# Gated DeltaNet and attention in one core: X^T of the inversion's levels 1 to 4 by VectorE's 32x32 transposes, and attention's matmuls in an order that alternates the halves of the array

## The chip, the cores and the metric

The kernel is one program on one NeuronCore of a Trainium2 chip. The metric is the device time in microseconds of one execution; lower is better. Engines are named as the profile names them: PE is TensorE's matmuls, PEld its weight loads, DVE is VectorE, ACT is ScalarE, POOL is GpSimd, SP is SyncE.

## What is computed

One inference step of a two-layer trunk, for 512 prompt tokens and 8 sequences of 8 sampled tokens (576 tokens together, 2048 channels). Layer 0 projects the normed input and splits the columns among sliding-window attention and a gated DeltaNet with 8 heads. The part of the DeltaNet that matters here solves, for each head and each chunk of tokens, a unit lower triangular system; the attention part is plain softmax attention with sinks.

```python
# gated DeltaNet, per head and chunk
lower = jnp.tril(jnp.einsum('...id,...jd->...ij', kb, kc) * decay, -1)
a_mat = lower + jnp.eye(c, dtype=f32)
sol = lax.linalg.triangular_solve(a_mat, rhs, left_side=True, lower=True, unit_diagonal=True)
...
# attention of the prompt, by blocks of 128 queries against 256 keys
s = jnp.einsum('...qhgd,...khd->...hgqk', q, k).astype(jnp.float32) * (HD_A ** -0.5)
...
return jnp.einsum('...hgqk,...khd->...qhgd', p.astype(v.dtype), v)
```

Layer 1 is a convolution module with its own projections; the change doesn't touch it.

## The kernel before

All activations lie with the channels on the partitions. The frame of the whole program is a stream of projection tiles: 133 weight tiles of 2048 x 128, each multiplied with the 576 tokens in 96 matmuls (16 blocks of 128 channels, 3 products of a high and a low part, 2 halves of the tokens). `proj(m, s, e)` issues one eighth of a tile: 12 matmuls with 288 columns. The weights are split on the chip: ACT writes `w_hi`, DVE writes `w_lo`.

Everything else of layer 0 is hung between these eighths by hand. `PE_PLAN` says after which eighth (slot) of a head's four tiles TensorE issues which step of the previous head's DeltaNet; `DVE_PLAN` and `ACT_PLAN` say at which slot VectorE and ScalarE come to theirs. The order on each engine is therefore fixed by the code, and semaphores that count steps (`pe_head`, `dve_head`, `act_head`, `pool_head`) connect the engines. Heads 0 and 7 are written out, heads 1 to 6 run in a loop of three rounds with two heads each.

The triangular matrices are inverted by doubling. X and its transpose are kept side by side in `xx[:, 0]` and `xx[:, 1]`, as four chunks of 128 x 128. After level l, X is block diagonal with blocks of 2^(l+1). Level l has three steps on TensorE, each with one eighth of a projection tile (12 matmuls) between it and the next:

- `a{l}` (L658): M_l times X, 4 matmuls of 128 columns, into bank 1 of `gp`. It waits for DVE's `X{l-1}`. ACT then copies it to `a1` (step `A{l}`).
- `x{l}`: the update of X, 4 matmuls of 64 columns with X^T as the weights (L666, bank 2, levels 1 to 5), and at once the update of X^T, 4 matmuls of 64 columns with `a1` as the weights (L669, bank 3, levels 1 to 6).
- DVE's `X{l}` subtracts both updates from the halves of `xx` that they touch (L1380, `full<-full,gp` of 128x256).

So `a{l}` and `x{l}` stand at every second slot, from slot 7 on. Between its `X{l}` steps DVE has the taps of the next head's short convolution (`arena<-arena,small`) and the `w_lo` halves.

Prompt attention has 16 units, each spread over three slots. In `att_scores` (L826) the two heads of a pair sit in partitions 0 to 63 and 64 to 127, so that a matmul uses 64 rows of the array; the first half's matmuls all go before the second half's, and each half writes its own bank. `att_turn` (L838) transposes the previous unit's probabilities, `att_weigh` (L846) multiplies them with V, with 64 columns of weights for either half. The weighing of the sampled tokens (L890 with the cached values, 128 rows; L892 with the new values, 8 rows) runs over the 8 sequences for one half of the columns and then for the other.

A float32 matmul is one instruction in the code and two in the trace (two weight loads and two matmuls).

Of the kernel before, what the change touches and what calls it, by code (L numbers as in the profile page):

```python
# [20 lines left out]
P = 128  # L21
# [58 lines left out]
class Tally:  # L80
# [15 lines left out]
    def leave(self, rounds):  # L96
# [5 lines left out]
LV = range(1, LEVELS)  # L102
PE_HEAD = (["kv_tok", "gcum", "norm", "gram", "m0"] + [f"{s}{i}" for i in LV for s in ("a", "x")]
           + ["u0", "so0"] + [f"{s}{c}" for c in range(1, NC) for s in ("s", "u", "so")] + ["o_chan"])
DVE_HEAD = (["kg", "dmask", "ssum", "vs", "Mt", "attn", "X", "Xt"] + [f"X{i}" for i in LV]
            + ["vp0", "S0", "o0"] + [f"{s}{c}" for c in range(1, NC) for s in ("r", "vp", "S", "o")]
            + ["on", "y"])
ACT_HEAD = ["sq", "decay"] + [f"A{i}" for i in LV] + [f"q{c}" for c in range(1, NC)] + ["osq"]
# [33 lines left out]
ACT_PLAN = {1: ["sq"], 2: ["decay"]} | {PE_AT[f"a{i}"]: [f"A{i}"] for i in LV}  # L142
ACT_PLAN |= {PE_AT[f"s{c}"]: [f"q{c}"] for c in range(1, NC)} | {30: ["osq"]}
DVE_PLAN = {1: ["kg"], 2: ["dmask"], 3: ["ssum"], 4: ["vs", "Mt", "attn"], 6: ["X", "Xt"]}
DVE_PLAN |= {PE_AT[f"x{i}"]: [f"X{i}"] for i in LV} | {PE_AT["u0"]: ["vp0"], PE_AT["so0"]: ["S0", "o0"]}
for _c in range(1, NC):
    DVE_PLAN |= {PE_AT[f"s{_c}"]: [f"r{_c}"], PE_AT[f"u{_c}"]: [f"vp{_c}"], PE_AT[f"so{_c}"]: [f"S{_c}", f"o{_c}"]}
DVE_PLAN |= {31: ["on"]}
# [47 lines left out]
def blk(c):  # L196

    return (c // 2) * HALF + (c % 2) * P


def hybrid_step(nc, x, wt, const, param, dn_prev, state_in, k_cache, v_cache, cf_prev,
                y, win_k, win_v, dn_out, dnc_out, cf_out, cfs_out, swk_out, swv_out, sdn_out):
    x1_dram = nc.dram_tensor("x1_scratch", (KT, P, TOK), F32, kind="Internal").ap()
    with ExitStack() as ctx:
# [29 lines left out]
        def half_blocks(ap, level, half):  # L234

            return ap.rearrange("p (n a b) -> p n a b", a=2, b=1 << level)[:, :, half, :]
# [284 lines left out]
        def _(pe):  # L521
# [99 lines left out]
            def head_step(it, kb, name):  # L621

                kt, qt, vt = kqv[kb][:, 0, :], kqv[kb][:, 1, :], kqv[kb][:, 2, :]
                ck = lambda c: slice(c * P, (c + 1) * P)
                if name == "kv_tok":
                    pe.wait_ge(conv_silu, 3 * it + 3)
                    if not (isinstance(it, int) and it == 0):
                        pe.wait_ge(dve_h.sem, dve_h.at("y", it - 1))
                    else:
                        pe.wait_ge(prep, 4)  # L630
                    for c in range(NC):
                        pe.transpose(gp[:, 0, ck(c)], kt[:, ck(c)], ident)
                    for c in range(NC):
                        ins = pe.transpose(gp[:, 1, ck(c)], vt[:, ck(c)], ident)
                elif name == "gcum":
                    pe.wait_ge(pool_h.sem, pool_h.at("gB", it))
                    for c in range(NC):
                        ins = pe.matmul(gp[:, 2, ck(c)], gB[:, c, :], tri, start=True, stop=True)
                elif name == "norm":
                    pe.wait_ge(act_h.sem, act_h.at("sq", it))  # L640
                    for c in range(8):
                        ins = pe.matmul(gp[:, 3, c:c + 1], sqkq_c[:, c, :], ones[:, 0:1], start=True, stop=True)
                elif name == "gram":
                    pe.wait_ge(dve_h.sem, dve_h.at("ssum", it))
                    for c in range(NC):
                        ins = pe.matmul(gp[:, 2 + c // 2, (c % 2) * 256:(c % 2) * 256 + 256], kt[:, ck(c)],
                                        kqv[kb][:, 0:2, ck(c)], start=True, stop=True)
                elif name == "m0":
                    pe.wait_ge(pool_h.sem, pool_h.at("L0", it))
                    pe.wait_ge(dve_h.sem, dve_h.at("vs", it))  # L650
                    for c in range(NC):
                        ins = pe.transpose(gp[:, 0, ck(c)], mtl[0][:, c, :], ident)
                elif name[0] == "a":
                    l = int(name[1])
                    pe.wait_ge(pool_h.sem, pool_h.at(f"L{l}", it))
                    pe.wait_ge(dve_h.sem, dve_h.at("Xt" if l == 1 else f"X{l - 1}", it))
                    for c in range(NC):
                        ins = pe.matmul(gp[:, 1, ck(c)], mtl[l % 2][:, c, :], xx[:, 0, c, :], start=True, stop=True)  # L658
                elif name[0] == "x":
                    l = int(name[1])  # L660
                    pe.wait_ge(act_h.sem, act_h.at(f"A{l}", it))
                    if l == 1:
                        pe.wait_ge(dve_h.sem, dve_h.at("attn", it))
                    if l < LEVELS - 1:
                        for c in range(NC):
                            pe.matmul(half_blocks(gp[:, 2, ck(c)], l, 0), xx[:, 1, c, :], half_blocks(a1[:, c, :], l, 0),  # L666
                                      start=True, stop=True)
                    for c in range(NC):
                        ins = pe.matmul(half_blocks(gp[:, 3, ck(c)], l, 1), a1[:, c, :],  # L669
                                        half_blocks(xx[:, 1, c, :], l, 1), start=True, stop=True)  # L670
                elif name == "o_chan":
                    pe.wait_ge(dve_h.sem, dve_h.at("on", it))
                    for c in range(NC):
                        ins = pe.transpose(gp[:, 0, ck(c)], on[:, c, :], ident)
                elif name[0:2] == "so":
                    c = int(name[2])
                    pe.wait_ge(dve_h.sem, dve_h.at(f"vp{c}", it))
                    pe.matmul(gp[:, 3, 0:P], kg[:, c, :], vp, start=True, stop=True)
                    ins = pe.matmul(gp[:, 0, 0:P], attn[:, c, :], vp, start=True, stop=True)
                elif name[0] == "s":  # L680
                    c = int(name[1])
                    pe.wait_ge(dve_h.sem, dve_h.at(f"o{c - 1}", it))
                    if c > 1:
                        pe.wait_ge(act_h.sem, act_h.at(f"q{c - 1}", it))
                    pe.matmul(gp[:, 0, 0:P], kt[:, ck(c)], st, start=True, stop=True)
                    ins = pe.matmul(gp[:, 1, 0:P], qt[:, ck(c)], st, start=True, stop=True)
                elif name[0] == "u":
                    c = int(name[1])
                    pe.wait_ge(dve_h.sem, dve_h.at(f"X{LEVELS - 1}" if c == 0 else f"r{c}", it))
                    ins = pe.matmul(gp[:, 2, 0:P], xx[:, 1, c, :], vs[:, 0, :] if c == 0 else rr,  # L690
                                    start=True, stop=True)
                ins.then_inc(pe_h.sem, 1)
# [120 lines left out]
            def att_scores(u):  # L813
                r, c, jj = u // 8, (u // 2) % 4, u % 2
                n = N_Q + 4 * r + 3
                pe.wait_ge(acc_free[n % 2], n // 2 + 1)
                if u == 0:
                    pe.wait_ge(vtok_done, 1)
                else:
                    pe.wait_ge(biased, u)  # L820
                for q in range(2):
                    rows = slice(64 * q, 64 * q + 64)
                    for j in range(2):
                        lhs = full[rows, 4 * r + 2 * jj + j, blk(c):blk(c) + P]
                        for w in range(0 if c else 1, 2):
                            ins = pe.matmul(gp[:, q, j * 256 + w * P:j * 256 + (w + 1) * P], lhs,  # L826
                                            kv[rows, 2 * r, blk(c - 1 + w):blk(c - 1 + w) + P],
                                            start=True, stop=True)
                ins.then_inc(scores, 1)
# [11 lines left out]
            def att_weigh(u):  # L841
                r, c = u // 8, (u // 2) % 4
                pe.wait_ge(turned_out, u + 1)
                for q in range(2):
                    for w in range(0 if c else 1, 2):
                        ins = pe.matmul(gp[64 * q:64 * q + 64, 2, 0:256], v_tok[:, c - 1 + w, r, 64 * q:64 * q + 64],  # L846
                                        probT[:, w, 2 * q:2 * q + 2, :], start=(w == (0 if c else 1)), stop=(w == 1))
                ins.then_inc(weighed, 1)

            def sampled_attention(name):  # L850
# [31 lines left out]
                elif name[0:5] == "weigh":  # L882
                    r = int(name[5])
                    pe.wait_ge(sa_act, SAA[f"v_new{r}"])
                    pe.wait_ge(vc_in, 16)
                    for q in range(2):
                        g = 2 * r + q
                        for b in range(NB):
                            o_ = gp[64 * q:64 * q + 64, 2, 0:256].rearrange("p (j b t) -> p b j t", j=4, b=NB)[:, b]
                            pe.matmul(o_, vc[:, b, 64 * g:64 * g + 64], probT_s[:, b, 32 * g:32 * g + 32],  # L890
                                      start=True, stop=False)
# [478 lines left out]
        def _(dve):  # L1370
# [157 lines left out]
            def head_dve(it, kb, name):  # L1528
# [30 lines left out]
                elif name[0] == "X":  # L1559
                    l = int(name[1])  # L1560
                    pe_at(f"x{l}")
                    for s_ in range(0 if l < LEVELS - 1 else 1, 2):
                        part = half_blocks(xx[:, s_].rearrange("p c t -> p (c t)"), l, s_)
                        ins = tt(part, part, half_blocks(gp[:, 2 + s_, :], l, s_), SUB)
                elif name[0:2] == "vp":
                    c = int(name[2])
                    pe_at(f"u{c}")
# [823 lines left out]
```

## Time and profile before

| | |
|---|---|
| time, 3 runs | 2173.59 us median (2172.85 to 2175.42) |
| the profiled execution | 2179.17 us, of which the span from the first to the last instruction is 2177.5 us |
| PE busy | 2095.1 us, 96% of the span, 15807 matmuls |
| DVE busy | 1165.7 us, 54% |
| ACT busy | 743.7 us, 34% |
| POOL busy | 699.8 us, 32% |
| mean DMA traffic | 85 GB/s |
| mean granted TensorE clock | 0.981 |

The projection tiles of layer 0 with the heads' steps run from about 50 to 710 us, the sampled tokens' DeltaNet to about 870 us, attention to about 1075 us. All times in the rows are microseconds from the start of the span, unless marked ns. A busy PE in this table only says that matmuls are in flight, since they overlap; what a group of matmuls costs is read as the distance from its first start to the start of what follows it.

### The profile page before, as it was taken

The numbers are of one execution on the slowest core, as the hardware profiler recorded it, in microseconds if no ns is written. First come the engines' busy times: TensorE is split into PE (matmuls) and PEld (weight loads), VectorE is DVE, ScalarE is ACT, GpSimd is POOL, SyncE is SP. The second block draws the span as 40 slices with busy tenths as digits, with TensorE's granted clock in tenths as the row PEclk, the third lists the DMA queues.
The fourth block names the chain that finished last, engine by engine and source line by source line (L and its number), as shares of the span: only waits on it lengthen the run. The fifth ranks groups of instructions, "written<-read, shape, count | busy, mean of one in ns | idle before, by whom it ended". The sixth has DMA issues, their size and how long they took to land. (4 is left out here: it accounts for less than half of the span.)

```text
span 2177.5 us, 41528 instructions
## 1 busy us (share of the span) xinstructions
PE 2095.1 (96%) x15807; PEld 2044.4 (94%) x15807; DVE 1165.7 (54%) x2148; ACT 743.7 (34%) x1228; POOL 699.8 (32%) x642
## 2 busy tenths in 40 slices
PE   4999999999999999999999999999999989999996
PEld 4999999999999988989899999999999989999996
DVE  6444544544543323565242237999999974462223
ACT  4322222222222211454232215555555533442220
POOL 3023123113213222100121116888888941021210
PEclk9999999999999999999899999999999999999998
DMA  5211111111111223411134323333333212223332
GB/s 175 89 40 60 60 52 53 56 59 51 58 51 65 71 97 121 145 50 59 41 123 143 127 91 85 89 94 101 87 96 92 70 62 94 77 69 119 109 113 92
DMA packets 74894, 184.24 MB, mean 85 GB/s; under 512 B 26360, under 2 KB 26680, under 8 KB 74536
## 3 DMA queue, kind: packets, MB, share of 16 engines
q1 hardware_dynamic: 66672, 163.58, 24.5%
q0 software_dynamic: 3504, 9.63, 1.4%
q10 hardware_dynamic: 4608, 9.44, 1.1%
q8 instruction: 84, 1.38, 0.3%
q14 instruction: 26, 0.21, 0.0%
HBM read 163.56 MB, written 19.06 MB: 84 GB/s over the span
## 5 line engine op out<-in xcount | busy, mean ns | idle before, releaser
L533 PE MATMUL acc<-act_hi,w_hi 128*128 128x288 f32 x4128 | 918.7, 304 | 16.4 <-DVE w_lo L1380 11.3
L533 PE MATMUL acc<-act_hi,w_lo 128*128 128x288 f32 x4128 | 890.4, 297 | 0.0
L533 PE MATMUL acc<-act_lo,w_hi 128*128 128x288 f32 x4128 | 888.9, 297 | 0.0
L533 PEld LDWEIGHTS acc<-act_hi,w_hi 128*128 128x128 f32 x4128 | 666.3, 191 | 33.3 <-issue 19.3
L533 PEld LDWEIGHTS acc<-act_lo,w_hi 128*128 128x128 f32 x4128 | 670.5, 190 | 0.0
L533 PEld LDWEIGHTS acc<-act_hi,w_lo 128*128 128x128 f32 x4128 | 670.2, 190 | 0.0
L1989 POOL TENSOR_TENSOR arena<-arena 128x512 f32<-128x512 f32 (+1 forms) x266 | 391.4, 1471 | 331.2 <-ACT arena L1245 285.1
L968 ACT ACTIVATE w_hi<-w_raw 128x1024 fp32r<-128x1024 f32 x266 | 279.9, 1055 | 449.6 <-PE acc L533 259.9
L1380 DVE TENSOR_TENSOR w_lo<-w_raw,w_hi 128x1024 fp32r<-128x1024 f32 x266 | 353.7, 1349 | 45.7 <-ACT w_hi L968 45.4
L1383 DVE SCALAR_TENSOR_TENSOR gp<-arena,par,gp 128x64 f32<-128x64 f32 (+1 forms) x688 | 248.2, 446 | 0.0
L968 ACT ACTIVATE arena<-arena,par 128x512 f32<-128x512 f32 x240 | 165.3, 720 | 98.5 <-POOL arena L1989 89.2
L968 ACT ACTIVATE arena<-gp 128x512 f32<-128x512 f32 (+4 forms) x86 | 50.9, 607 | 404.0 <-PE gp L658 257.9
L1380 DVE TENSOR_TENSOR full<-acc,arena 128x576 f32 (+1 forms) x32 | 24.2, 757 | 274.3 <-PE acc L533 274.3
L1989 POOL TENSOR_TENSOR arena<-arena,cst 128x24 f32<-128x24 f32 (+5 forms) x84 | 41.3, 503 | 364.2 <-ACT arena L968 179.1
L1380 DVE TENSOR_TENSOR full<-full,gp 128x256 f32<-128x256 f32 (+1 forms) x104 | 45.0, 469 | 179.4 <-PE gp L669 179.4
L1989 POOL TENSOR_TENSOR act_lo<-full,act_hi 128x576 fp32r<-128x576 f32 x32 | 58.3, 1838 | 168.9 <-ACT act_hi L968 168.9
L1989 POOL TENSOR_TENSOR full<-full,cst 128x512 f32<-128x512 f32 x56 | 79.1, 1424 | 56.8 <-PE gp L658 33.8
L1989 POOL TENSOR_TENSOR small<-small 128x4 f32<-128x4 f32 (+4 forms) x84 | 45.2, 543 | 148.8 <-DVE small L1387 84.3
L1383 DVE SCALAR_TENSOR_TENSOR arena<-arena,small 128x512 f32<-128x512 f32 (+2 forms) x145 | 68.5, 515 | 0.0
L1383 DVE SCALAR_TENSOR_TENSOR arena<-arena,acc 128x576 f32<-128x576 f32 x24 | 18.0, 751 | 81.3 <-ACT arena L1326 75.2
L658 PE MATMUL gp<-full 128*128 128x128 f32 x384 | 51.3, 277 | 2.7 <-DVE full L1380 2.7
L658 PEld LDWEIGHTS gp<-full 128*128 128x128 f32 x384 | 47.6, 191 | 4.6 <-DVE full L1380 3.6
(246 smaller groups left out, 1664.5 us busy)
## 6 DMA issues: line engine op xcount, KB each, us to landing
w_raw<-wt SPq DMA_DIRECT2D x266, 512.0 KB, 3.9
full<-x SPq DMA_DIRECT2D x8, 576.0 KB, 8.7
arena<-x SPq DMA_DIRECT2D x16, 288.0 KB, 3.3
x_scratch<-full ACTq DMA_DIRECT2D x16, 288.0 KB, 3.9
arena<-x_scratch SPq DMA_DIRECT2D x16, 288.0 KB, 2.8
out_y<-full ACTq DMA_DIRECT2D x16, 288.0 KB, 2.4
arena<-state_in SPq DMA_DIRECT2D x6, 512.0 KB, 4.2
out_sdn<-arena POOLq DMA_DIRECT2D x6, 512.0 KB, 3.0
```

The source lines that it names most:

```text
L533: ins = pe.matmul(acc[:, s, i, 0:HALF], w[:, s, wk], a[:, k, i * HALF:(i + 1) * HALF], start=(k == 0 and j == 0), stop=(k == KT - 1 and j ...
L658: ins = pe.matmul(gp[:, 1, ck(c)], mtl[l % 2][:, c, :], xx[:, 0, c, :], start=True, stop=True)
L968: return act.activation(out, in_, ACT.Copy, scale=scale)
L1380: return dve.tensor_tensor(out, a, b, op)
L1383: return dve.scalar_tensor_tensor(out=out, in0=a, scalar=scalar, in1=b, op0=op0, op1=op1)
L1989: return pool.tensor_tensor(out, a, b, op)
```

## The change

For levels 1 to 4 X^T isn't updated by its own product any more. TensorE leaves out L669's matmuls there, DVE updates only `xx[:, 0]`, and a new DVE step `T{l}` transposes all four chunks of X in blocks of 32x32 into `xx[:, 1]`. Up to level 4 X has no entry outside its diagonal blocks of 32, so this is its whole transpose. TensorE's `x{l}` waits for the `T{l-1}` before it. Levels 5 and 6 are as before, and so is the sampled tokens' inversion. In attention the loops are turned so that successive matmuls alternate between the two halves of the array.

```diff
@@ plans
-DVE_HEAD = (["kg", "dmask", "ssum", "vs", "Mt", "attn", "X", "Xt"] + [f"X{i}" for i in LV]
+IN_BLOCKS = range(1, 5)
+DVE_HEAD = (["kg", "dmask", "ssum", "vs", "Mt", "attn", "X", "Xt"]
+            + [n for i in LV for n in [f"X{i}"] + [f"T{i}"] * (i in IN_BLOCKS)]
@@ TensorE, head_step, x{l}
                     if l == 1:
                         pe.wait_ge(dve_h.sem, dve_h.at("attn", it))
+                    else:
+                        pe.wait_ge(dve_h.sem, dve_h.at(f"T{l - 1}" if l - 1 in IN_BLOCKS else f"X{l - 1}", it))
                     if l < LEVELS - 1:
                         for c in range(NC):
-                            pe.matmul(half_blocks(gp[:, 2, ck(c)], l, 0), xx[:, 1, c, :], half_blocks(a1[:, c, :], l, 0),
-                                      start=True, stop=True)
-                    for c in range(NC):
-                        ins = pe.matmul(half_blocks(gp[:, 3, ck(c)], l, 1), a1[:, c, :],
-                                        half_blocks(xx[:, 1, c, :], l, 1), start=True, stop=True)
+                            ins = pe.matmul(half_blocks(gp[:, 2, ck(c)], l, 0), xx[:, 1, c, :],
+                                            half_blocks(a1[:, c, :], l, 0), start=True, stop=True)
+                    if l not in IN_BLOCKS:
+                        for c in range(NC):
+                            ins = pe.matmul(half_blocks(gp[:, 3, ck(c)], l, 1), a1[:, c, :],
+                                            half_blocks(xx[:, 1, c, :], l, 1), start=True, stop=True)
@@ TensorE, att_scores
-                for q in range(2):
-                    rows = slice(64 * q, 64 * q + 64)
-                    for j in range(2):
-                        lhs = full[rows, 4 * r + 2 * jj + j, blk(c):blk(c) + P]
-                        for w in range(0 if c else 1, 2):
-                            ins = pe.matmul(gp[:, q, j * 256 + w * P:j * 256 + (w + 1) * P], lhs,
+                for j in range(2):
+                    for w in range(0 if c else 1, 2):
+                        for q in range(2):
+                            rows = slice(64 * q, 64 * q + 64)
+                            ins = pe.matmul(gp[:, q, j * 256 + w * P:j * 256 + (w + 1) * P],
+                                            full[rows, 4 * r + 2 * jj + j, blk(c):blk(c) + P],
@@ TensorE, att_weigh
-                for q in range(2):
-                    for w in range(0 if c else 1, 2):
+                for w in range(0 if c else 1, 2):
+                    for q in range(2):
@@ TensorE, weighing of the sampled tokens
-                    for q in range(2):
-                        g = 2 * r + q
-                        for b in range(NB):
+                    for b in range(NB):
+                        for q in range(2):
+                            g = 2 * r + q
@@ VectorE, head_dve
-                    for s_ in range(0 if l < LEVELS - 1 else 1, 2):
+                    for s_ in range(0 if l < LEVELS - 1 else 1, 1 if l in IN_BLOCKS else 2):
                         part = half_blocks(xx[:, s_].rearrange("p c t -> p (c t)"), l, s_)
                         ins = tt(part, part, half_blocks(gp[:, 2 + s_, :], l, s_), SUB)
+                elif name[0] == "T":
+                    dve.wait_ge(dve_h.sem, dve_h.at(f"X{name[1]}", it))
+                    ins = dve.transpose(xx[:, 1].rearrange("p c t -> p (c t)"), xx[:, 0].rearrange("p c t -> p (c t)"))
```

`DVE_PLAN` puts each `T{l}` behind its `X{l}` in the same slot. The lines of the changed kernel stand 2 to 5 further down, so L533, L666 and L1380 of before are L535, L670 and L1385 of the change.

TensorE's order at `x1` of a head, before (L533 is a projection eighth, `gp<-arena,full` the update of X, `gp<-full,arena` that of X^T):

```order
L533 MATMUL acc<-act_lo,w_hi 128x288 x2
L533 MATMUL acc<-act_hi,w_lo 128x288 x2
L666 MATMUL gp<-arena,full 128x32x2 x4
L669 MATMUL gp<-full,arena 128x32x2 x4
L533 MATMUL acc<-act_hi,w_hi 128x288 x2
L533 MATMUL acc<-act_lo,w_hi 128x288 x2
```

And in the change:

```order
L535 MATMUL acc<-act_lo,w_hi 128x288 x2
L535 MATMUL acc<-act_hi,w_lo 128x288 x2
L670 MATMUL gp<-arena,full 128x32x2 x4
L535 MATMUL acc<-act_hi,w_hi 128x288 x2
L535 MATMUL acc<-act_lo,w_hi 128x288 x2
```

The four matmuls of X^T are gone, and the next projection eighth follows those of X; nothing else moves on TensorE around them.

VectorE's order at `X1` to `X3` of the same head, before (`full<-full,gp` is an update of `xx`, `arena<-arena,small` a tap of the convolution):

```order
L1380 TENSOR_TENSOR full<-full,gp 128x128x2 x2
L1380 TENSOR_TENSOR w_lo<-w_raw,w_hi 128x1024
L1380 TENSOR_TENSOR full<-full,gp 128x64x4 x2
L1387 TENSOR_SCALAR arena<-arena,small 128x512
L1387 TENSOR_SCALAR arena<-arena,small 128x64
L1383 SCALAR_TENSOR_TENSOR arena<-arena,small 128x512
L1383 SCALAR_TENSOR_TENSOR arena<-arena,small 128x64
L1380 TENSOR_TENSOR full<-full,gp 128x32x8 x2
```

And in the change:

```order
L1385 TENSOR_TENSOR full<-full,gp 128x128x2
L1572 STREAM_TRANSPOSE full<-full 128x512
L1385 TENSOR_TENSOR w_lo<-w_raw,w_hi 128x1024
L1385 TENSOR_TENSOR full<-full,gp 128x64x4
L1572 STREAM_TRANSPOSE full<-full 128x512
L1392 TENSOR_SCALAR arena<-arena,small 128x512
L1392 TENSOR_SCALAR arena<-arena,small 128x64
L1388 SCALAR_TENSOR_TENSOR arena<-arena,small 128x512
L1388 SCALAR_TENSOR_TENSOR arena<-arena,small 128x64
L1385 TENSOR_TENSOR full<-full,gp 128x32x8
```

One of the two updates gives way to a transpose of all 512 columns, ahead of the `w_lo` half and the taps that follow in the same slot.

## Rows read from the trace of the kernel before

**Rows 1.** Who waited for whom on PE over the span, longest in total first.

```profile
PE acc L533 <- issue: 5.1, 2, 2.6
PE gp L658 <- DVE full L1380: 2.7, 8, 0.4
```

**Rows 2.** Stages (heads; sampled weighing): us, PE, PEld, DVE, ACT, POOL busy, granted clock.

```profile
110.00:420.00 310.00, 304.85 (x2388) 301.67 (x2386) 150.77 (x308) 79.20 (x158) 73.23 (x114) 0.99 0.17 55
...
1040.00:1075.00 35.00, 35.00 (x242) 31.39 (x241) 7.38 (x13) 3.44 (x4) 0.57 (x1) 0.80 0.10 32
```

**Rows 3.** PE's groups: busy time, mean ns of one.

```profile
L669 PE MATMUL gp<-full,arena 128*128 128x64 f32 x384 | 50.3, 273 | 0.0
...
L826 PE MATMUL gp<-arena,full 64*128 64x128 f32 x224 | 23.4, 286 | 0.0
...
L846 PE MATMUL gp<-arena 128*64 128x256 f32 x112 | 15.7, 394 | 0.0
```

**Rows 4.** PE in order of time, levels 1 and 2 of a head: start, length.

```profile
440.25 1.00 PE L666 MATMUL gp<-arena,full 128*128 128x64 f32 x8
...
441.95 0.50 PE L533 MATMUL acc<-act_hi,w_hi 128*128 128x288 f32 x2
...
443.62 1.05 PE L658 MATMUL gp<-full 128*128 128x128 f32 x8
444.43 0.51 PE L533 MATMUL acc<-act_hi,w_hi 128*128 128x288 f32 x2
...
446.11 1.00 PE L666 MATMUL gp<-arena,full 128*128 128x64 f32 x8
```

**Rows 5.** DVE in order of time, same head: start, length, [idle before <-releaser].

```profile
442.19 0.75 DVE L1380 TENSOR_TENSOR full<-full,gp 128x256 f32<-128x256 f32 x2 [4.58 <-PE gp L669]
...
459.76 0.75 DVE L1380 TENSOR_TENSOR full<-full,gp 128x256 f32<-128x256 f32 x2 [2.25 <-PE gp L669]
...
470.58 0.42 DVE L1380 TENSOR_TENSOR full<-full,gp 128x256 f32<-128x256 f32 x1 [3.07 <-PE gp L669]
```

**Rows 6.** DVE's groups, SBUF to SBUF with 512 columns: busy time, mean ns of one.

```profile
L1387 DVE TENSOR_SCALAR arena<-arena,small 128x512 f32<-128x512 f32 x24 | 11.6, 483 | 8.9 <-ACT arena L968 8.9
...
L1380 DVE TENSOR_TENSOR full<-cst,full 128x512 f32<-128x512 f32 x8 | 9.2, 1149 | 0.0
```

**Rows 7.** PE in order of time, attention: a unit with 8 score matmuls.

```profile
931.43 1.71 PE L826 MATMUL gp<-arena,full 64*128 64x128 f32 x16
933.07 1.09 PE L838 MATMUL gp<-cst,arena 128*128 128x128 f32 x8
```

**Rows 8.** PE's matmuls begun by 931.97, 932.00, 940.10 and 928.65.

```profile
931.43 0.71 PE L826 MATMUL gp<-arena,full 64*128 64x128 f32 x4
...
931.43 0.93 PE L826 MATMUL gp<-arena,full 64*128 64x128 f32 x6
...
940.09 0.39 PE L826 MATMUL gp<-arena,full 64*128 64x128 f32 x2
...
928.62 0.45 PE L846 MATMUL gp<-arena 128*64 128x256 f32 x2
```

**Rows 9.** PE in order of time, sampled weighing, where one column half gives way to the other.

```profile
1045.16 0.30 PE L892 MATMUL gp<-arena 8*64 8x32 f32 x2
1045.38 0.30 PE L890 MATMUL gp<-arena 128*64 128x32 f32 x2
1045.62 0.30 PE L892 MATMUL gp<-arena 8*64 8x32 f32 x2
```

**Rows 10.** DVE in order of time, the probabilities of units 2 and 15.

```profile
896.41 1.23 DVE L1380 TENSOR_TENSOR arena<-arena,small 128x1024 f32<-128x1024 f32 x1
...
1004.25 1.23 DVE L1380 TENSOR_TENSOR arena<-arena,small 128x1024 f32<-128x1024 f32 x1
```

**Rows 11.** PE in order of time, the transposes of those probabilities.

```profile
898.48 0.44 PE L838 MATMUL gp<-cst,arena 128*128 128x128 f32 x2
...
1005.53 0.44 PE L838 MATMUL gp<-cst,arena 128*128 128x128 f32 x2
```

More of the change, by code:

```diff
@@ L144 @@
 DVE_PLAN = {1: ["kg"], 2: ["dmask"], 3: ["ssum"], 4: ["vs", "Mt", "attn"], 6: ["X", "Xt"]}
-DVE_PLAN |= {PE_AT[f"x{i}"]: [f"X{i}"] for i in LV} | {PE_AT["u0"]: ["vp0"], PE_AT["so0"]: ["S0", "o0"]}
+DVE_PLAN |= {PE_AT[f"x{i}"]: [f"X{i}"] + [f"T{i}"] * (i in IN_BLOCKS) for i in LV} | {PE_AT["u0"]: ["vp0"], PE_AT["so0"]: ["S0", "o0"]}
 for _c in range(1, NC):
```

## The prediction

> **What bounds the kernel now.** I read the time first, then the stages, then who waits for whom, and last single groups of matmuls in order of time. PE is in flight for 304.85 of 310 us in the heads' stage, while DVE is busy for 150.77, ACT and POOL for less than 80 each [rows 2]. What the heads' PE waits for is small: the chain of waits shows 2.7 us over 8 occasions for DVE at `a1` (L658) and two pauses of together 5.1 us with no cause in the profile, in projection matmuls [rows 1]. No wait at all is recorded at L666, L669, L826, L838, L846 or L890. So in the two stages that the change touches TensorE sets the pace, and what is taken from its stream shortens the span one for one, as long as nobody else becomes late by it. The mean duration of one matmul is no price: L669 has 384 of them at 273 ns, 104.8 us by that, while the group is in flight for 50.3 us only [rows 3]. The price is the distance between starts.
>
> **X^T without its matmuls.** L669's 384 matmuls are 8 heads x 6 levels x 4 chunks x 2 records [rows 3], so levels 1 to 4 take out 256 of them, in 32 groups of 8. In a level as it is, L666 starts at 440.25 and the projection goes on at 441.95: 1.70 us for 16 records. A group of 8 by itself is `a2`: L658 starts at 443.62, the projection at 444.43, that is 0.81 us [rows 4]. The two have different widths (64 and 128 columns) and nearly the same pace (0.106 and 0.101 us a record), so width sets no price here and 0.81 is right for the L666 group that remains. A level saves 1.70 - 0.81 = 0.89 us, and 32 levels **28.5 us**. From below I bound the saving by 8 records at 0.101 us, 25.9 us in all.
>
> DVE's side: an `X{l}` step now makes one update instead of two, 0.42 instead of 0.75 us [rows 5], so it gives back 0.33 us. It gains a transpose of 128x512 from SBUF to SBUF, which this trace doesn't show. The nearest rows with the same size, both of SBUF alone, are the `TENSOR_SCALAR` at 483 ns and the `TENSOR_TENSOR` with two inputs beside a busy POOL at 1149 ns [rows 6]; it reads one tensor and writes one, so it is nearer to the first, and with the wait for its own `X{l}` I take 0.7 us, from 0.5 to 1.3. DVE's balance at a level: the shortest idle time before such a step is 2.25 us, at `X4` [rows 5]. The level gets shorter by 0.89, the step longer by 0.7 - 0.33 = 0.37: 0.99 us of idle time stay. The `w_lo` half and the taps behind the transpose start 0.37 us later after `x{l}` than now, and find that idle time again before the next step. That cover is worth naming: with a transpose of more than about 1.7 us DVE would no longer be waiting at `X4`.
>
> PE's side: `a{l+1}` still waits for `X{l}` only. DVE begins it at 442.19 and has it 0.42 later, at 442.61, while `a2` starts at 443.62 [rows 4, 5]; today both updates are ahead of it, so this wait gets looser by 0.33 us. New is the wait of `x{l+1}` for `T{l}`. Queued behind it are the 4 matmuls of L666 and with them all projections. From the end of `x1` at 441.95 to `x2` at 446.11 there are 4.16 us, which the change leaves as they are. Of these, 0.24 pass until DVE starts and 0.42 with X, so 3.5 us are there for a transpose of 0.7. I price it at nothing.
>
> The Trainium skill ("VectorE: DVE Perf Modes", The three transpose paths) gives 311 ns for a VectorE transpose of 128x128 bf16 and says that it transposes 32x32 blocks only. An estimate from it for four such chunks is 1.24 us, under both limits, so the sum would be the same; no row here shows it.
>
> **Attention's scores.** 12 of the 16 units have 8 score matmuls (16 records), 4 have 4. In one of the 12 the group starts at 931.43 and what follows at 933.07: 1.64 us [rows 7]. Looking closer, by 931.97 four records had begun, in 0.54 us, and by 932.00 six, so that the second half's stream enters at about 931.98 and from there both run beside each other [rows 8]. In a short unit two records begin within 10 ns, at 940.09 [rows 8]: there the second half is near enough in the queue to start with the first. So the array already runs both halves at once where it sees them. Alternating, the second stream starts with the first in the long units too, 0.55 us earlier (931.98 - 931.43), and the group ends as much earlier: 12 x 0.55 = **6.6 us**. The short units gain nothing. Bounds: nothing, and half of 1.64 us in all 12, 9.8 us.
>
> **Attention's weighing.** In `att_weigh` two records of L846 begin within 30 ns of its start at 928.62 [rows 8]: only the halves' separate streams can do that, so they already run together and another order gives **nothing**. In the sampled weighing a pair of L890 (128 rows) and a pair of L892 (8 rows) follow one another at 0.23 us, and where one column half gives way to the other, at 1045.38, the distances are 0.22 and 0.24, the same [rows 9]. If another half were enough to overlap, this place would be closer. The new order has the same number of changes between 128 and 8 rows, so I take **nothing** again. On the other side, with both halves beside each other: 32 blocks (2 pairs of heads, 2 halves, 8 sequences) of 0.46 us are 14.7 us, and half of that is 7.4 us.
>
> Here the Trainium skill speaks both ways. "TensorEngine Tiling (Array Packing)", Key Properties, says that different tiles can load and multiply in parallel, and that changing the tiling mode drains TensorE. By the first alone the sampled weighing would halve; by the second its changes of rows keep it as it is. The trace agrees with the second, with its 0.22 to 0.24 us at the change of half.
>
> **Who could be late in attention.** DVE finishes the probabilities of unit 2 at 897.64 and PE turns them at 898.48; for unit 15 it is 1005.48 and 1005.53 [rows 10, 11]. Between the end of a unit's scores and its turn lies the next unit's score group, so the first slack, 0.84, shrinks by 0.55 to 0.29. The second doesn't shrink, as no score group lies in between: it stays at 0.05. Nothing new is late, but the cover is thin in both.
>
> **The sum.** 28.5 + 6.6 = 35.1 us. The profiled execution took 2179.17 us for a span of 2177.5, so it would take 2144.1; it is 5.6 us above the median of the runs, 2173.59. Taken from the median: **2138.5 us**, 1.6% faster.
>
> **Rivals.**
> 1. *The scores gain nothing*, because alternating halves reload weights in a way that the two streams of today don't. Against it stand the short units [rows 8]. Time: 2173.59 - 28.5 = 2145.1. Chance 0.07.
> 2. *Alternating column halves also pays in the sampled weighing*, since a block of 128 and 8 rows of one half could run beside that of the other: the 7.4 us from above go too. For it speaks that L846 overlaps [rows 8], against it the change of half in rows 9. Time 2138.5 - 7.4 = 2131.1. Chance 0.06. (It is the first of the two rules that the Trainium skill's "TensorEngine Tiling (Array Packing)" gives under Key Properties.)
> 3. *TensorE's clock.* The 35 us around the sampled weighing were granted 0.80 of full speed, so 14 of them ran at 1.2 instead of 2.4 GHz, which is 7 us lost [rows 2]. These stretches shift with everything before them, and the change takes out work of the array. One of half that length more or less is 3.5 us: 2135 or 2142. This is part of the likeliest case's width, not a case of its own.
> 4. *The transpose holds TensorE up: slower.* `x{l+1}` stalls for what a transpose takes beyond 3.5 us, in 32 places. The gain is gone when each stalls 35.1 / 32 = 1.1 us, that is from 4.6 us on; with 5.0 us the stalls cost 48 us and the time is 2187. For it speaks only that no row shows the operation, against it that 4.6 us is four times the slower neighbour in rows 6. A transpose of 3.5 to 4.6 us would leave part of the gain, or none. Chance 0.03 for slower, 0.02 for no change, 0.03 for a part of the gain (2150 to 2165).
>
> The likeliest case, as summed, has 0.79. Its own range is 2132 to 2145: the lower bound of a level's saving adds 2.6 us, the clock 3.5 to either side. To hold the time 8 times in 10 I go from 2130, which takes in rival 2, to 2148, which takes in rival 1 with its clock. A measurement can tell this kernel from no change at about 0.2%, 4.3 us. Faster by more than that: 0.79 + 0.07 + 0.06 + 0.03 = 0.95; within it 0.02; slower 0.03.
>
> **What the profile of the changed kernel would show.** Right: 15551 matmuls; L670 followed by a projection 0.81 us after its start; a head's period shorter by 3.6 us; no waits at `x{l}`; 32 transposes of 0.5 to 1.3 us; long score groups of 1.09 us whose second record pair begins within 20 ns of the first; weighing groups as long as before. Wrong: waits at L670 for DVE L1572; score groups still of 1.64 us; waits at the turns (L838's counterpart) for DVE, which would mean that the thin cover is gone and part of the 6.6 us came back as a wait.

## The result, and the profile after

The changed kernel takes 2141.29 us (median of 4 runs, 2141.03 to 2144.38), against 2173.22 us (2172.24 to 2175.42) for the kernel before on the same chip. The ratio is 0.9855, with an interval of 0.9838 to 0.9872: 31.9 us less, 28 to 35 by the interval. The prediction was 2138.5 us, in a range of 2130 to 2148. The profiled execution took 2141.03 us for a span of 2139.3.

The page of the changed kernel begins like this:

```profile
span 2139.3 us, 41080 instructions
PE 2056.4 (96%) x15551; PEld 2005.9 (94%) x15551; DVE 1176.5 (55%) x2148; ACT 743.7 (35%) x1228; POOL 701.2 (33%) x642
```

256 matmul records are gone (128 matmuls in the code), and PE is in flight for 38.7 us less than the 2095.1 of before. Its share is 96% still: that share can't show a gain, as said ahead of the prediction. DVE has 10.8 us more: 22.8 of transposes came, and 32 updates of X^T went.

These are the groups of the changed kernel with each shape apart (busy time, mean ns of one, idle time before and what ended it):

```profile
L670 PE MATMUL gp<-arena,full 128*128 128x64 f32 x320 | 40.0, 267 | 0.0
L674 PE MATMUL gp<-full,arena 128*128 128x64 f32 x128 | 16.5, 271 | 0.0
L1385 DVE TENSOR_TENSOR full<-full,gp 128x256 f32<-128x256 f32 x56 | 22.9, 420 | 138.6 <-PE gp L670 81.4 <-PE gp L674 57.2
L1572 DVE STREAM_TRANSPOSE full<-full 128x512 f32<-128x512 f32 x32 | 22.8, 711 | 1.1
```

L674 is what is left of L669 [rows 3]: 128 records for levels 5 and 6. L670, the update of X, now waits for a transpose at four levels of each head (`x2` to `x5`), and its idle time is 0.0. The operation that no row of before showed takes 711 ns.

One head in order of time. On TensorE, levels 1 and 2 (start, length in flight):

```profile
424.75 1.00 PE L670 MATMUL gp<-arena,full 128*128 128x64 f32 x8
425.56 0.51 PE L535 MATMUL acc<-act_hi,w_hi 128*128 128x288 f32 x2
...
429.73 1.00 PE L670 MATMUL gp<-arena,full 128*128 128x64 f32 x8
```

On VectorE, level 1 and then level 4 of the same head (in brackets the idle time before):

```profile
425.79 0.42 DVE L1385 TENSOR_TENSOR full<-full,gp 128x256 f32<-128x256 f32 x1 [3.68 <-PE gp L670]
426.25 0.71 DVE L1572 STREAM_TRANSPOSE full<-full 128x512 f32<-128x512 f32 x1
...
440.71 0.42 DVE L1385 TENSOR_TENSOR full<-full,gp 128x256 f32<-128x256 f32 x1 [0.98 <-PE gp L670]
```

Against [rows 4] this reads as follows. The update group takes 0.81 us from its start to the projection's (424.75 to 425.56), where the two groups took 1.70. The level's period, from `x1` to `x2`, is 4.98 us (424.75 to 429.73), where it was 5.86 (440.25 to 446.11): 0.88 us less, and 32 times 0.88 is 28.2. At `X4`, where DVE had 2.25 us to spare [rows 5], it has 0.98.

In attention, a unit with 8 score matmuls, and below it how far the group had come by 887.83:

```profile
887.80 1.16 PE L830 MATMUL gp<-arena,full 64*128 64x128 f32 x16
888.90 0.44 PE L843 MATMUL gp<-cst,arena 128*128 128x128 f32 x2
...
887.80 0.38 PE L830 MATMUL gp<-arena,full 64*128 64x128 f32 x2
```

The group takes 1.10 us instead of the 1.64 of [rows 7], and its second record starts within 0.03 us of the first, where in [rows 8] the second half came in after 0.55. Twelve such units give 12 x 0.54 = 6.5 us. A long group of `att_weigh` takes 1.02 us (885.00 to 886.02), where before it took 1.03 (902.67 to 903.70). The sampled weighing stays as it was too. Pairs of records with 128 rows (L895) and with 8 rows (L897) follow each other at 0.23 us, as in [rows 9], though the half of the columns now changes after every two pairs:

```profile
1006.64 0.30 PE L895 MATMUL gp<-arena 128*64 128x32 f32 x2
1006.87 0.30 PE L897 MATMUL gp<-arena 8*64 8x32 f32 x2
1007.10 0.38 PE L895 MATMUL gp<-arena 128*64 128x32 f32 x2
```

### The profile page after: what moved, and what is told of

The parts are those of the page before. It is cut to its first block, busy times and chain, and to the rows that moved or that the text cites. A ratio compares the mean times of both kernels' runs of the same rounds, so it can differ in the third digit from the quotient of the medians.

```text
span 2139.3 us, 41080 instructions
## 1 busy us (share of the span) xinstructions
PE 2056.4 (96%) x15551; PEld 2005.9 (94%) x15551; DVE 1176.5 (55%) x2148; ACT 743.7 (35%) x1228; POOL 701.2 (33%) x642
## 4 chain that ended last, share of the span: by engine, by line
PE 41%; DVE 4%; issue 4%; POOL 1%; ACT 1%; DMA 0%; POOLq 0%; DVEq 0%; ACTq 0%; SPq 0%
PE acc L535 40%; DVE full L1388 1%; DVE full L1385 1%; POOL arena L1997 1%; DVE act_lo L1385 1%; DVE w_lo L1385 1%; PE acc L563 0%; DMA w_raw<-wt 0%; PE gp L592 0%; ACT arena L973 0%; PE gp L577 0%; DVE arena L1388 0%; ACT w_hi L973 0%; ACT act_hi L973 0%; DVE arena L1385 0%
## 5 line engine op out<-in xcount | busy, mean ns | idle before, releaser
L535 PE MATMUL acc<-act_hi,w_hi 128*128 128x288 f32 x4128 | 917.2, 304 | 17.4 <-DVE w_lo L1385 10.8
L535 PE MATMUL acc<-act_hi,w_lo 128*128 128x288 f32 x4128 | 889.2, 297 | 0.0
L535 PE MATMUL acc<-act_lo,w_hi 128*128 128x288 f32 x4128 | 888.1, 297 | 0.0
L535 PEld LDWEIGHTS acc<-act_hi,w_hi 128*128 128x128 f32 x4128 | 664.8, 191 | 33.2 <-issue 19.8
L535 PEld LDWEIGHTS acc<-act_lo,w_hi 128*128 128x128 f32 x4128 | 669.4, 190 | 1.1 <-issue 1.1
L535 PEld LDWEIGHTS acc<-act_hi,w_lo 128*128 128x128 f32 x4128 | 669.4, 190 | 0.0
L1385 DVE TENSOR_TENSOR w_lo<-w_raw,w_hi 128x1024 fp32r<-128x1024 f32 x266 | 353.0, 1347 | 43.9 <-ACT w_hi L973 43.6
L1385 DVE TENSOR_TENSOR full<-acc,arena 128x576 f32 (+1 forms) x32 | 24.2, 757 | 275.5 <-PE acc L535 275.5
L1385 DVE TENSOR_TENSOR full<-full,gp 128x256 f32<-128x256 f32 (+1 forms) x72 | 34.3, 493 | 138.6 <-PE gp L670 81.4
L660 PE MATMUL gp<-full 128*128 128x128 f32 x384 | 51.3, 277 | 2.7 <-DVE full L1385 2.7
L660 PEld LDWEIGHTS gp<-full 128*128 128x128 f32 x384 | 47.5, 191 | 4.6 <-DVE full L1385 3.6
```

The lines of the kernel that those rows point to most:

```text
L535: ins = pe.matmul(acc[:, s, i, 0:HALF], w[:, s, wk], a[:, k, i * HALF:(i + 1) * HALF], start=(k == 0 and j == 0), stop=(k == KT - 1 and j ...
L1385: return dve.tensor_tensor(out, a, b, op)
```

## The experiments

**The parts by themselves.** The theory is the prediction's: 28.5 us from the matmuls that go, 6.6 from the scores, nothing from either weighing. The rivals: the level's gain comes from the new waits or from DVE's shorter step rather than from TensorE's stream; or the weighing loops take part in it. Three kernels undo parts, and the changed kernel runs beside them, against 19 runs of the kernel before (2177.99 us, 2174.05 to 2181.08). The kernel with only the heads' part:

```diff
@@ att_scores (att_weigh and the sampled weighing likewise as before)
-                for j in range(2):
-                    for w in range(0 if c else 1, 2):
-                        for q in range(2):
+                for q in range(2):
+                    for j in range(2):
+                        for w in range(0 if c else 1, 2):
```

The kernel before with only the new order of the scores has this loop the other way round and nothing else of the change. The third keeps transposes and waits, and issues the X^T matmuls all the same. They write bank 3, from which nobody reads at these levels:

```diff
-                    if l not in IN_BLOCKS:
+                    if l:
```

Expected of the changed kernel once more:

> The changed kernel once more, beside the kernel before. Theory (both edits only shorten TensorE's stream; 28.4 us in the heads and 6.4 us in the scores, as the trace of after shows): 33 to 36 us faster if the 31.9 us of the first timing was short by the granted clock's chance; rival (3 us of the two gains are really given back somewhere): 31 to 33 us again.

Of the heads' part alone:

> Only the first half of the change: X^T by transposes, attention's matmuls in the order of before. Theory: 28.4 us faster than before (about 2145). Rival (the two halves of the change get in each other's way and lose about 3 us together): 30 us or more here, or the scores alone give more than their 6.5.

Of the scores' order alone:

> Only att_scores alternates between the halves of the array; the weighings and the heads are those of before. Theory: 12 groups shorter by 0.55 us, so 6.5 us faster (about 2167), and all of attention's gain is here. Rival (the weighings' new order has a part in it): less than 5 us.

Of the change with the matmuls kept:

> The changed kernel, but TensorE still computes the update of X^T at levels 1 to 4 into bank 3, where nobody reads it. Theory (the heads' gain is TensorE's time and nothing else): the 28.4 us are gone and attention's 6.5 stay, about 2167. Rival (the gain comes from VectorE's shorter or earlier X step, which frees the steps after it): about 2141 as the changed kernel.

| kernel | median, us | range | ratio to before |
|---|---|---|---|
| changed kernel | 2144.42 | 2141.66 to 2144.88 | 0.9842 (0.9829 to 0.9854) |
| heads' part only | 2148.21 | 2147.23 to 2152.5 | 0.9870 (0.9855 to 0.9884) |
| scores' order only | 2170.04 | 2166.95 to 2177.41 | 0.9969 (0.9956 to 0.9982) |
| change, matmuls kept | 2172.38 | 2160.0 to 2176.35 | 0.9968 (0.9955 to 0.9982) |

The parts add up, taken by the ratios: 28.3 us (1.30%) from the heads and 6.8 (0.31%) from the scores are 1.61%, the whole is 1.58%. Each interval is about 3 us to either side. With only the scores turned 6.8 us are there, so no gain of more than those 3 us is left for either weighing's new order, and the traces show both weighings at their old pace. With transposes and waits in place but the matmuls kept, what remains is 7.0 us, the scores' part. The heads' gain is the matmuls: within the interval neither the transposes nor the shorter `X{l}` move the time. The trace of that kernel shows the old level:

```profile
439.39 1.00 PE L670 MATMUL gp<-arena,full 128*128 128x64 f32 x8
440.23 1.05 PE L674 MATMUL gp<-full,arena 128*128 128x64 f32 x8
...
445.24 1.00 PE L670 MATMUL gp<-arena,full 128*128 128x64 f32 x8
```

5.85 us from `x1` to `x2`, as in [rows 4]. The score groups say the same. In the kernel with only the scores turned, then in the one with only the heads' part:

```profile
921.92 1.16 PE L825 MATMUL gp<-arena,full 64*128 64x128 f32 x16
923.01 1.09 PE L838 MATMUL gp<-cst,arena 128*128 128x128 f32 x8
```

```profile
882.61 1.71 PE L831 MATMUL gp<-arena,full 64*128 64x128 f32 x16
884.25 0.98 PE L843 MATMUL gp<-cst,arena 128*128 128x128 f32 x7
```

The distance between the two rows is 1.09 us in the first and 1.64 in the second.

**How long a transpose may be.** The prediction let the slower rival begin at 3.5 us per transpose and eat the whole gain at 4.6. To test that, each `T{l}` is preceded by 2, 4 or 5 copies of itself, which do the same work again. The edit is written here with `n` for the number of transposes, 3, 5 or 6; `DVE_PLAN` gets the same names:

```diff
-            + [n for i in LV for n in [f"X{i}"] + [f"T{i}"] * (i in IN_BLOCKS)]
+            + [s for i in LV for s in [f"X{i}"] + [f"Y{i}{k}" for k in range(n - 1) if i in IN_BLOCKS] + [f"T{i}"] * (i in IN_BLOCKS)]
...
-                elif name[0] == "T":
-                    dve.wait_ge(dve_h.sem, dve_h.at(f"X{name[1]}", it))
+                elif name[0] in "TY":
+                    dve.wait_ge(dve_h.sem, dve_h.at(name, it) - 1)
```

Three in a row:

> Every T step does its transpose three times, one after the other, each waiting for the one before: about 2.3 us instead of 0.71. Theory (TensorE needs the transpose only 3.5 us after X): no wait of TensorE at x2 to x5, the time of the changed kernel, 2141, although VectorE is no longer waiting at X4. Rival (VectorE's queue is already full, what comes after X4 gets late): 2145 or more.

Six in a row:

> The same with six transposes, about 4.5 us. Theory as in the prediction (a stall of what goes beyond 3.5 us, in 32 places): 1 us x 32 = 32 us, about 2173. Rival (VectorE itself becomes the pace, since X, six transposes, taps and w_lo are 6 to 8 us in a level of 5 us): the lateness adds up over the levels, 2180 or more.

And, once those two were known, five:

> Five transposes in every T step, about 3.7 us with the waits between them. By the prediction's limit of 3.5 us a stall of 0.2 us in 32 places, 6 us, so about 2149. By what six transposes did (67 us lost for 1 us beyond the limit at each place, with VectorE's lateness added up over the levels and the clock lower in the heads' stage): 2150 to 2180, with waits of TensorE for the T steps of the later levels first.

Each ratio is taken against the kernel before on the same chip (medians of 2177.99, 2177.10, 2176.41 and 2177.10 us).

| kernel | time in transposes at a level | median, us | ratio to before |
|---|---|---|---|
| changed kernel | 0.71 us | 2144.42 | 0.9842 (0.9829 to 0.9854) |
| three | 2.20 us | 2142.13 | 0.9839 (0.9823 to 0.9854) |
| five | 3.70 us | 2171.89 | 0.9980 (0.9967 to 0.9992) |
| six | 4.44 us | 2209.53 | 1.0150 (1.0134 to 1.0166) |

Three cost nothing. VectorE's timeline with three, at level 4, shows no idle time ahead of `X4` any more, and still no wait of L670 for a transpose is recorded:

```profile
441.61 0.41 DVE L1385 TENSOR_TENSOR full<-full,gp 128x256 f32<-128x256 f32 x1
442.05 2.20 DVE L1572 STREAM_TRANSPOSE full<-full 128x512 f32<-128x512 f32 x3
```

Five, at 3.70 us, should by the prediction's sum have cost 0.2 us at 32 places, some 6 us. They cost about 30 us by the ratios, nearly the whole gain. Six, at 4.44 us, should have left 5 us of the gain; the kernel is 32.4 us slower than before, and by the ratios 67 slower than the changed kernel. The waits at L670 that the two traces record (for whom, us in total, times, longest), five first and then six:

```profile
PE gp L670 <- DVE full L1572: 9.9, 20, 1.0
```

```profile
PE gp L670 <- DVE full L1572: 35.6, 29, 1.8
```

The place is as predicted, the size isn't. VectorE's timeline with five, in levels 1 to 4 of a head, shows why:

```profile
439.57 0.42 DVE L1385 TENSOR_TENSOR full<-full,gp 128x256 f32<-128x256 f32 x1 [3.67 <-PE gp L670]
...
444.92 0.42 DVE L1385 TENSOR_TENSOR full<-full,gp 128x256 f32<-128x256 f32 x1
...
450.38 0.41 DVE L1385 TENSOR_TENSOR full<-full,gp 128x256 f32<-128x256 f32 x1
450.83 3.69 DVE L1572 STREAM_TRANSPOSE full<-full 128x512 f32<-128x512 f32 x5
454.45 0.91 DVE L1388 SCALAR_TENSOR_TENSOR arena<-arena,small 128x512 f32<-128x512 f32 x2
455.27 1.22 DVE L1385 TENSOR_TENSOR w_lo<-w_raw,w_hi 128x1024 fp32r<-128x1024 f32 x1
456.41 0.94 DVE L1388 SCALAR_TENSOR_TENSOR arena<-arena,small 128x512 f32<-128x512 f32 x2
457.27 0.41 DVE L1385 TENSOR_TENSOR full<-full,gp 128x256 f32<-128x256 f32 x1
```

and TensorE's update groups `x1` to `x5`, with the one recorded wait at an `a{l}` between them:

```profile
438.53 1.00 PE L670 MATMUL gp<-arena,full 128*128 128x64 f32 x8
...
443.78 1.10 PE L670 MATMUL gp<-arena,full 128*128 128x64 f32 x8
...
449.13 1.10 PE L670 MATMUL gp<-arena,full 128*128 128x64 f32 x8
...
454.58 1.10 PE L670 MATMUL gp<-arena,full 128*128 128x64 f32 x8 [0.23 <-DVE full L1572]
...
457.74 1.16 PE L660 MATMUL gp<-full 128*128 128x128 f32 x8 [0.41 <-DVE full L1385]
...
461.47 1.10 PE L670 MATMUL gp<-arena,full 128*128 128x64 f32 x8 [0.99 <-DVE full L1572]
```

At `X1` VectorE still begins on time, 1.04 us after `x1` (438.53 to 439.57), and there the rule of the prediction nearly holds: TensorE's level takes 5.25 us (438.53 to 443.78) for 4.98, 0.27 more where the rule said 0.2. Behind it no row of VectorE has idle time before it. From `X2` to `X3` its queue takes 5.46 us (444.92 to 450.38) and from `X3` to `X4` 6.89 (450.38 to 457.27), while TensorE would need 4.98. `X4` begins 2.69 us after its update group (454.58 to 457.27), where in the changed kernel an `X` step begins 1.04 after it (424.75 to 425.79). The lateness is handed from one level to the next, by the taps and `w_lo` halves that stand between the transposes. TensorE's levels grow with it: 5.35, 5.45 and 6.89 us. In the last of them `X4` is late enough for `a5` to wait too, 0.41 us at L660. The four levels together are 3.02 us longer than 4 x 4.98; an estimate for eight such heads is 24 us, and this execution is 20.9 us longer than the traced one of the changed kernel (2165.39 against 2144.45). The level of 5.35 us is 0.37 us too long without a wait in its row: `x3` starts at 449.13, 0.05 us after the transposes ended at 449.08, while matmuls from before were in flight until 449.00. So the recorded idle time of PE is a lower bound for what a late release costs.

The granted clock is second to this. The heads' stage of the changed kernel, then that of the one with six transposes (us, PE, PEld, DVE, ACT and POOL busy, clock, DMA share, GB/s):

```profile
110.00:670.00 560.00, 548.68 (x4271) 542.48 (x4270) 293.45 (x568) 149.88 (x294) 142.22 (x213) 1.00 0.18 58
```

```profile
110.00:670.00 560.00, 516.37 (x3803) 503.50 (x3803) 365.76 (x653) 132.61 (x260) 124.53 (x190) 0.96 0.16 51
```

0.96 over 560 us is 45 us at 1.2 GHz instead of 2.4, or 22 us lost, a third of the 67. TensorE had short gaps there; that these brought the clock down was not tested by itself. With five transposes the clock of this stage is 0.99, which is at most 6 of the 30 us.

**Runs of two in the scores.** Does the second half's stream start at once with runs of two, as it seems to where a unit has only four matmuls [rows 8]? The loops go j, q, w instead of j, w, q:

> The score matmuls alternate in runs of two (both key blocks of one query block for half 0, then for half 1) instead of one by one. Theory (the second half starts with the first when it stands no more than 4 records behind): long groups of 1.09 us as in the changed kernel. Rival (only strict alternation overlaps from the start): between 1.09 and 1.64 us.

```profile
868.93 1.26 PE L830 MATMUL gp<-arena,full 64*128 64x128 f32 x16
870.12 0.55 PE L843 MATMUL gp<-cst,arena 128*128 128x128 f32 x3
...
868.93 0.39 PE L830 MATMUL gp<-arena,full 64*128 64x128 f32 x2
```

The one run took 2150.29 us, and one run can't tell 1 us; the trace can. The last row shows how far the group had come by 869.00: two records, so the second half's stream starts at once, as with strict alternation. In this the theory was right. Its time for the group was not: it takes 1.19 us, between 1.10 of strict alternation and 1.64 of no alternation. The 0.1 us is lost in the second half of the group; by 0.5 us both orders had begun 8 records. Four records of one half ahead of the other do not keep the second stream back, eight do, by 0.55 us. Strict alternation is best, by 0.1 us a group; why was not tested.

**Why the sampled weighing gains nothing.** The prediction's reason was that each pair changes the number of rows, 128 and 8, and that this keeps the halves apart. If so, the alternation should pay as soon as nearly all those changes are gone. All 128-row matmuls of a pair of heads now go first, then all 8-row ones; the first matmul of each half opens the accumulation and the last closes it:

```diff
-                    for b in range(NB):
-                        for q in range(2):
-                            ...
-                            pe.matmul(o_, vc[...], probT_s[...], start=True, stop=False)
-                            ins = pe.matmul(o_, v_new[...], probT_n[...], start=False, stop=True)
+                    for part in range(2):
+                        for b in range(NB):
+                            for q in range(2):
+                                ...
+                                if part == 0:
+                                    pe.matmul(o_, vc[...], probT_s[...], start=(b == 0), stop=False)
+                                else:
+                                    ins = pe.matmul(o_, v_new[...], probT_n[...], start=False, stop=(b == NB - 1))
```

A second kernel has `for q` outside `for b`, which takes the alternation away again.

> The sampled weighing takes all 16 matmuls of 128 rows first and then all 16 of 8 rows, both alternating between the halves, instead of changing the number of rows 32 times. Theory (the changes of rows are what keeps the halves apart): each of the two blocks falls from 8.7 us to 2 to 4 us, 9 to 13 us faster than the changed kernel, about 2130. Rival (the 128 and 8 rows by themselves have that pace): each block stays above 7 us.

> The sampled weighing with all 128-row matmuls first and all 8-row ones after them, but one column half after the other instead of alternating. Theory (with the changes of rows gone, halves run beside each other only where they alternate): each of the two blocks takes 3 to 4 us, longer than the 2.1 us of the alternating one and far below the 8.5 us of the changed kernel. Rival (grouping alone does it, the order of the halves is nothing): 2.1 us.

TensorE in order of time, first of the two pairs of heads. Grouped and alternating:

```profile
1007.22 1.13 PE L897 MATMUL gp<-arena 128*64 128x32 f32 x32
1008.28 1.12 PE L900 MATMUL gp<-arena 8*64 8x32 f32 x32
1009.33 0.53 PE L535 MATMUL acc<-act_hi,w_hi 128*128 128x288 f32 x2
```

Grouped, the halves one after the other:

```profile
1006.88 1.84 PE L897 MATMUL gp<-arena 128*64 128x32 f32 x32
1008.66 1.84 PE L900 MATMUL gp<-arena 8*64 8x32 f32 x32
1010.43 0.40 PE L535 MATMUL acc<-act_hi,w_hi 128*128 128x288 f32 x1
```

The same 64 records take 2.11 us grouped and alternating, 3.55 grouped with the halves apart, and 8.74 in the changed kernel. At 3.55 us a pair of records takes 0.11 us; with a change of rows it takes 0.23 at the same clock. So a change costs about 0.12 us, and there is one per pair. The grouped kernels also put the two matmuls that add into one target further apart and open and close accumulations less often. The shared target isn't the cause: in the changed kernel the step from L897 to the next L895 goes to another target and takes 0.23 us as well (1006.87 to 1007.10). Opening and closing by itself was not tested. At 0.23 us, 32 pairs would take 7.4 us; in the changed kernel the distance grows from 0.23 to 0.35 us after 1007.10, and so the block comes to 8.74 (1002.52 to 1011.26): the lower of TensorE's two clocks, 1.2 GHz, has set in. The Trainium skill ("TensorEngine Tiling (Array Packing)", Key Properties) says that a change of mode drains TensorE and that different tiles can run in parallel. The traces agree with both, if a change of the number of rows is such a change of mode: 0.12 us for each change, and 3.55 down to 2.11 us for the halves beside each other. That the array is drained at it no row here shows.

The stretch from 1000 to 1040 us, in the changed kernel and in the grouped one:

```profile
1000.00:1040.00 40.00, 40.00 (x269) 36.31 (x268) 7.38 (x13) 3.77 (x5) 0.57 (x1) 0.79 0.14 42
```

```profile
1000.00:1040.00 40.00, 36.66 (x369) 35.29 (x367) 13.86 (x19) 11.17 (x16) 7.35 (x6) 1.00 0.19 56
```

The lower clock behind the weighing [rows 2] is gone too; with the halves apart the same stretch was granted 0.96. The grouped kernel takes 2127.11 us (2126.16 to 2129.17), ratio 0.9772 (0.9758 to 0.9785) to the kernel before at 2177.10: 50 us less than that one, and by the ratios 15 less than the changed kernel. It beats both. Two blocks of 6.63 us less are 13.3 us of it; the projections behind them, no longer at the lower clock, gain some more. With the halves apart one run took 2132.49 us.

## Why the prediction was right, and where it was off

- **TensorE sets the pace, and the price is the distance between starts.** Right. A level lost 0.88 us of 0.89 forecast; the part alone measured 28.3 us against 28.5, and with the matmuls put back only the scores' part was left.
- **VectorE's side.** Right, with 711 ns for the 0.7 taken and 0.98 us of idle time at `X4` for the 0.99 forecast. The closeness of the first is partly luck: the 0.7 was a neighbour's 0.48 with an allowance for the wait, chosen from 0.5 to 1.3, and the operation alone takes 0.71. The Trainium skill ("VectorE: DVE Perf Modes", The three transpose paths) gives 311 ns for 128x128 in bf16. The estimate of 1.24 us, four times that, was too high: measured, 128x512 of float32 takes 0.71.
- **PE's new wait priced at nothing.** Right for this transpose: L670 has 0.0 us idle.
- **Scores.** Right: 1.10 us for 1.09, 12 units, and 6.8 us in the part alone for 6.6, with an interval of 3.9 to 9.6.
- **Both weighings at nothing.** Right, and the reason given, that changes of rows keep the halves apart, is borne out by the grouped kernels, with the opening and closing of accumulations as the rival that is left. `att_weigh` was not tried by itself; its groups take 1.02 us for 1.03.
- **Thin covers in attention.** Half right. Unit 2 and unit 15 had no wait, and unit 2's slack is 0.28 us (864.33 to 864.61) for the 0.29 forecast. But the turn of unit 12 came to wait about 0.2 us, for probabilities that ended at 943.09. First VectorE there, then TensorE at the turn:

```profile
935.15 1.22 DVE L1385 TENSOR_TENSOR w_lo<-w_raw,w_hi 128x1024 fp32r<-128x1024 f32 x1
936.28 1.22 DVE L1388 SCALAR_TENSOR_TENSOR arena<-gp,cst 128x1024 f32<-128x1024 f32 x1
...
941.87 1.22 DVE L1385 TENSOR_TENSOR arena<-arena,small 128x1024 f32<-128x1024 f32 x1
```

```profile
943.15 0.33 PE L843 MATMUL gp<-cst,arena 128*128 128x128 f32 x1
```

  A `w_lo` half had got in ahead of the unit's bias step. The prediction looked at two units of 16 and named the right kind of wait at the wrong one.
- **The slower rival's size: the step that failed.** The prediction said that "`x{l+1}` stalls for what a transpose takes beyond 3.5 us" and that the gain is gone "from 4.6 us on". Measured, nearly all of the gain is gone at 3.7 us, and at 4.44 the kernel is slower by 1.5%. It measured the room between one `X{l}` and the `x{l+1}` behind it as if VectorE always began on time. At the first level, where it does, five transposes cost 0.27 us for 0.2; over four levels 3.02 for 0.8. It had the other limit, 1.7 us until VectorE stops waiting at `X4`, and did not carry it on: beyond it the budget is VectorE's whole queue over a head, not the gap at a level. Between 2.2 us, which is free, and 3.7 the price rises steeply. For a transpose of 0.7 us this changed nothing but the rival's margin.
- **The sum.** 35.1 us forecast; 31.9 measured in the first batch and 33.6 in the second (34.4 by the ratio), with intervals that reach to 35 and 37. The traces' parts make 28.2 + 6.5 = 34.7. Whether up to 3 us are missing can't be told here: the runs of one kernel spread by 3 to 16 us, and where TensorE runs at its lower clock shifts from kernel to kernel. It stays open.

## What to carry to other kernels

Price a removed or reordered group of matmuls by the distance from its first start to the start of what follows, not by the mean duration of one. Work moved to an engine with idle time is free only until the shortest idle time between its steps is used up; beyond that, add up that engine's queue over the whole stage, since lateness is handed on from step to step. Here the halves of the array ran beside each other when their matmuls alternated and the number of rows stayed the same (2.11 us against 3.55 and 8.74); so try grouping matmuls by their number of rows first, then alternating.

## What the hardware showed that was not expected

- Changing between 128 and 8 rows at every matmul cost 0.12 us a time. Grouping 64 records by rows took 8.74 us (in part at the lower clock) down to 3.55, and alternating them as well down to 2.11. The two together give more than the alternation of the scores gave in all 12 units (6.5 us).
- In the scores, 8 records of one half ahead of the other kept the second stream back by 0.55 us; 4 did not keep it back, and yet the group took 1.19 us against 1.10 in strict alternation.
- The granted clock over the sampled weighing, 0.79, went to 1.00 when the same matmuls were issued grouped and alternating, and to 0.96 grouped with the halves apart. In the changed kernel the distance between pairs grew within the block, after some 20 of its 32 pairs; the grouped block was over in 2.11 us.
